# A diagonal recurrence step: product pair and sum on four instructions, rewritten as one product, one reduction and one copy

## What is computed

```python
def s5_direction(u, lam_re, lam_im, log_dt, b_c, h0):
    ...
    a_bar = jnp.exp(lam * dt)
    bu = jnp.einsum('gpc,blgc->blgp', b_bar, u.astype(jnp.complex64))
    bu = bu.at[:, 0].add(a_bar[None] * h0)
    _, h = lax.associative_scan(_lin_combine, (a, bu), axis=1)     # h[t] = a_bar * h[t-1] + bu[t]
    return h
```

## Time and profile before

| | us |
|---|---|
| median of 2 timed runs | 3121.78 (3121.66 to 3121.9) |
| the profiled execution | 3101.36 |
| its span, slowest core (core 0) | 3099.8 |
| spans of the eight cores | 3076.8 to 3099.8 |
| DVE busy, whole span | 1417.5 (46%) |
| ACT busy | 1153.7 (37%) |
| TensorE busy | 1255.5 (41%) |
| POOL busy | 216.6 (7%) |

### The profile page before, as it was taken

How to read it: one execution, slowest core, us unless ns; L and a number is a source line. 1 busy time by engine, 2 the same in 40 slices (tenths; PEclk the granted TensorE clock), 3 DMA queues, 4 the chain that set the end, 5 groups by cost and what they waited for, 6 DMA issues and landing times.

```text
span 3099.8 us, 31698 instructions; the slowest of 8 cores (3076.8 to 3099.8 us)
## 1 busy us (share of the span) xinstructions
PE 1255.5 (41%) x7855; PEld 731.2 (24%) x7855; DVE 1417.5 (46%) x2898; ACT 1153.7 (37%) x1628; POOL 216.6 (7%) x636
## 2 busy tenths in 40 slices
PE   2212162010344646524366706202035463688753
PEld 1211150000223333212132305000032342333332
DVE  1468315666234656275432422566522556523333
ACT  2131524444544343213332333444454534333233
POOL 1000002222000010000000000222200001000000
PEclk9985576565667566667687857556567665699877
DMA  8133210000000100112243241000001011022312
GB/s 210 43 82 82 88 50 31 1 1 1 18 22 12 40 12 31 55 53 70 82 130 105 99 140 45 24 1 1 7 11 31 10 34 37 26 68 75 109 67 96
DMA packets 148798, 162.53 MB, mean 52 GB/s; under 512 B 32872, under 2 KB 124680, under 8 KB 146824
## 3 DMA queue, kind: packets, MB, share of 16 engines
q1 hardware_dynamic: 148616, 160.51, 17.5%
HBM read 119.99 MB, written 40.50 MB: 52 GB/s over the span
## 4 chain that ended last, share of the span: by engine, by line
DVE 32%; PE 25%; issue 14%; DMA 13%; ACT 13%; DVEq 2%; SPq 1%; POOL 1%; ACTq 0%; POOLq 0%
PE ps L1083 7%; DVE T L781 4%; DVE T L779 4%; DVE E L783 4%; ACT wbf L308 3%; PE ps L1086 3%; DVE ors L1041 3%; DMA wst<-w_in 2%; DMA wst<-w_mod 2%; PE ps L1055 2%; PE ps L911 2%; PE ps L901 2%; PE ps L1125 2%; PE ps L702 2%; DVEq L59 2%
## 5 line engine op out<-in xcount | busy, mean ns | idle before, releaser
L782 ACT CAST bufB<-E 128x64 bf16<-128x64 f32 x512 | 242.2, 476 | 318.1 <-DVE T L781 318.0
L1083 PE MATMUL ps<-hT,wbf 128*128 128x512 bf16 x1024 | 263.7, 404 | 172.5 <-ACT wbf L308 169.5
L778 POOL TENSOR_TENSOR T<-E,A 128x64 f32<-128x64 f32 x512 | 163.5, 319 | 1405.9 <-DVE E L776 984.0
L308 ACT CAST wbf<-wst 128x2048 bf16<-128x2048 f32 (+1 forms) x84 | 135.0, 1621 | 213.9 <-DMA wst<-w_in 91.7
L1088 ACT ACTIVATE sg<-ps 128x512 f32<-128x512 f32 x128 | 76.4, 597 | 296.5 <-PE ps L1083 248.9
L759 PE MATMUL ps<-hT,wbf 128*128 128x512 bf16 x256 | 63.7, 415 | 298.6 <-ACT wbf L308 298.6
L1083 PEld LDWEIGHTS ps<-hT,wbf 128*128 128x128 bf16 x1024 | 103.5, 103 | 308.9 <-issue 205.1
L783 DVE TENSOR_TENSOR E<-T,T 128x64 f32<-128x64 f32 x512 | 115.7, 226 | 120.0 <-DVE T L781 87.4
L781 DVE TENSOR_TENSOR T<-T,bufB 128x64 f32<-128x64 f32 x512 | 136.8, 267 | 54.4 <-DVE T L779 1.9
L815 PE MATMUL ps<-GT,bufB 128*128 128x128 bf16 x256 | 43.5, 261 | 284.1 <-ACT Bt L790 284.1
L779 DVE TENSOR_TENSOR T<-E,A 128x64 f32<-128x64 f32 x512 | 116.6, 228 | 54.4 <-DVE E L783 1.9
(11 more groups left out here) (247 smaller groups left out, 2946.7 us busy)
## 6 DMA issues: line engine op xcount, KB each, us to landing
wst<-w_in SPq DMA_DIRECT2D x32, 1024.0 KB, 7.0
wst<-w_mod SPq DMA_DIRECT2D x24, 1024.0 KB, 7.4
xo<-xs_scr SPq DMA_DIRECT2D x8, 2048.0 KB, 10.9
xin<-x SPq DMA_DIRECT2D x16, 512.0 KB, 18.0
xs_scr<-xt SPq DMA_DIRECT2D x4, 2048.0 KB, 12.9
wst<-w_o SPq DMA_DIRECT2D x8, 1024.0 KB, 6.0
xs_scr<-xo SPq DMA_DIRECT2D x4, 2048.0 KB, 17.6
y<-yout SPq DMA_DIRECT2D x16, 512.0 KB, 2.6
```

The lines of the kernel that those rows point to most:

```text
L308: mk.op("act", lambda e: e.copy(bfv, stv), reads=["wst%d" % i], writes=["wbf%d" % j])
L778: mk.op("pool", lambda e, cur=cur: e.tensor_tensor(T1[:], cur, A1[:], ALU.mult), reads=[ck, "A1"], writes=["T1"])
L782: mk.op("act", lambda e, i=i, cur=cur: e.copy(V(Eb, RL, i, [[NR, 64]]), cur), reads=[ck], writes=[ks])
L1083: mk.op("pe", lambda e, ps1=ps1, kt=kt, tt=tt, oc2=oc2, wm=wm: e.matmul(ps1[:], wm[:, kt, oc2 * 128:(oc2 + 1) * 128], hT_ap(kt, tt * 512, ...
```

## The change

The state is kept as three runs of 32 columns, real, imaginary and real again, in `SBF`, so that the swapped state is a window into the same tile that starts 32 columns later. `A12` holds A1 and A2 side by side. One DVE product then makes both products (128 columns) into the first two thirds of `GX`. ACT copies X[i] into the last third (`xprefetch`), one step ahead. A DVE reduction adds the three thirds, and a DVE copy renews the second real run. POOL has no part in the loop any more. The entry blend every 32 steps is followed by the same copy.

```diff
--- before.py
+++ after.py
@@ -736,14 +736,16 @@
                 mk.barrier()
                 dump("Xb", Xb[:], "Xb")
                 ckpt("X")
-                E2 = sb("E2", [128, 128], F32, ph)
-                T1 = sb("T1", [128, 64], F32, ph)
-                T2 = sb("T2", [128, 64], F32, ph)
+                SBF = sb("SBF", [128, 2 * 96], F32, ph)
+                GX = sb("GX", [128, 2 * 192], F32, ph)
+                A12 = sb("A12", [128, 128], F32, ph)
                 EX = sb("EX", [128, NSEG * 64], F32, ph)
                 OST = sb("OST", [128, NSEG * 64], F32, ph)
                 mk.dma(EX[:], s5ext_d.ap()[l], writes=["EX"])
-                memset("dve", E2[:], 0.0, "E2_0")
+                memset("dve", SBF[:], 0.0, "E2_0")
                 mk.bufs["E2_1"] = {"w": mk.bufs["E2_0"]["w"], "r": {}}
+                mk.op("dve", lambda e: e.tensor_copy(A12[:, 0:64], A1[:]), reads=["A1"], writes=["A12"])
+                mk.op("dve", lambda e: e.tensor_copy(A12[:, 64:128], A2[:]), reads=["A2"], writes=["A12"])
                 RL = NR * 64
                 sgtA = [sb("sgtA%d" % i_, [128, 512], BF16, ph) for i_ in range(2)]
 
@@ -763,26 +765,36 @@
                                 yield
 
                 gagen = gate_a_gen()
+
+                def xprefetch(i):
+                    go = (i % 2) * 192
+                    mk.op("act", lambda e, i=i, go=go: e.copy(GX[:, go + 128: go + 192], V(Xb, RL, i, [[NR, 64]])), reads=["Xs%d" % i], writes=["GXx%d" % (i % 2)])
+
+                xprefetch(0)
                 for i in range(NR):
                     if i % max(1, NR // 16) == 0:
                         pump(gagen)
                     kb = i // 32
-                    co = (i % 2) * 64
-                    no = ((i + 1) % 2) * 64
+                    co = (i % 2) * 96
+                    no = ((i + 1) % 2) * 96
+                    go = (i % 2) * 192
                     ck, nk = "E2_%d" % (i % 2), "E2_%d" % ((i + 1) % 2)
-                    cur = E2[:, co:co + 64]
+                    gk, gxk = "GXg%d" % (i % 2), "GXx%d" % (i % 2)
                     ks = "Xs%d" % i
                     if i % 32 == 0:
-                        mk.op("dve", lambda e, cur=cur, kb=kb: e.scalar_tensor_tensor(cur, cur, flags[:, 1:2], EX[:, kb * 64:(kb + 1) * 64], ALU.mult, ALU.add),
+                        mk.op("dve", lambda e, co=co, kb=kb: e.scalar_tensor_tensor(SBF[:, co:co + 64], SBF[:, co:co + 64], flags[:, 1:2], EX[:, kb * 64:(kb + 1) * 64], ALU.mult, ALU.add),
                               reads=[ck, "flags", "EX"], writes=[ck])
-                    mk.op("pool", lambda e, cur=cur: e.tensor_tensor(T1[:], cur, A1[:], ALU.mult), reads=[ck, "A1"], writes=["T1"])
-                    mk.op("dve", lambda e, co=co: e.tensor_tensor(V(T2, 64, 0, [[32, 2], [1, 32]]), V(E2, 128, co + 32, [[-32, 2], [1, 32]]), V(A2, 64, 0, [[32, 2], [1, 32]]), ALU.mult),
-                          reads=[ck, "A2"], writes=["T2"])
-                    mk.op("dve", lambda e, i=i: e.tensor_tensor(T2[:], T2[:], V(Xb, RL, i, [[NR, 64]]), ALU.add), reads=["T2", ks], writes=["T2"])
-                    mk.op("act", lambda e, i=i, cur=cur: e.copy(V(Eb, RL, i, [[NR, 64]]), cur), reads=[ck], writes=[ks])
-                    mk.op("dve", lambda e, no=no: e.tensor_tensor(E2[:, no:no + 64], T1[:], T2[:], ALU.add), reads=["T1", "T2"], writes=[nk])
+                        mk.op("dve", lambda e, co=co: e.tensor_copy(SBF[:, co + 64:co + 96], SBF[:, co:co + 32]), reads=[ck], writes=[ck])
+                    mk.op("dve", lambda e, co=co, go=go: e.tensor_tensor(V(GX, 384, go, [[64, 2], [1, 64]]), V(SBF, 192, co, [[32, 2], [1, 64]]), V(A12, 128, 0, [[64, 2], [1, 64]]), ALU.mult),
+                          reads=[ck, "A12"], writes=[gk])
+                    mk.op("act", lambda e, i=i, co=co: e.copy(V(Eb, RL, i, [[NR, 64]]), SBF[:, co:co + 64]), reads=[ck, gxk], writes=[ks])
+                    if i + 1 < NR:
+                        xprefetch(i + 1)
+                    mk.op("dve", lambda e, no=no, go=go: e.tensor_reduce(SBF[:, no:no + 64], V(GX, 384, go, [[1, 64], [64, 3]]), mybir.AxisListType.X, ALU.add),
+                          reads=[gk, gxk], writes=[nk])
+                    mk.op("dve", lambda e, no=no: e.tensor_copy(SBF[:, no + 64:no + 96], SBF[:, no:no + 32]), reads=[nk], writes=[nk])
                     if (i + 1) % 32 == 0:
-                        mk.op("act", lambda e, kb=kb, no=no: e.copy(OST[:, kb * 64:(kb + 1) * 64], E2[:, no:no + 64]), reads=[nk], writes=["OST"])
+                        mk.op("act", lambda e, kb=kb, no=no: e.copy(OST[:, kb * 64:(kb + 1) * 64], SBF[:, no:no + 64]), reads=[nk], writes=["OST"])
                 drain(gagen)
                 mk.dma(s5o_d.ap()[l], OST[:], reads=["OST"])
                 mk.barrier()
```

## The result

The changed kernel takes 3168.5 us, the median of 11 runs, against 3103.6 us, the median of 10 runs of the kernel before measured with it. The ratio is 1.020, with a 95% interval of 1.016 to 1.024: some 65 us slower. The forecast was slower by 119.6 us. The direction was right, the forecast growth nearly double the measured one. (The base of the forecast, 3121.8 us, was a median of two runs; ten put it at 3103.6, so the growth is what is compared here.) The ratio leaves out slow runs, three of the 11 (3227.9 to 3246.2 us, with a lower granted clock on cores 0 to 3) and one of the 10 before (3150.8 us).

A forecast was written before the change was run, and what follows sets the result against it. The recurrence was taken as bound by DVE's serial chain: +0.225 us a step times 512 gave +115.2, block starts +4.4, together +119.6 us on a base of 3121.8: 3241.4 us, range 3168 to 3268.

The forecast's parts named there:

- What bounds the stage: Recurrence: bound by latency, only DVE's serial chain counts, 1.10 us a step, paid 512 times.
- POOL's removal saves nothing: Recurrence step: POOL's product, 0.32 us, was hidden, so taking it out gains nothing.
- Product 128x128: New DVE product in each step: 292 ns, bounds 228 and 374.
- Reduction: New DVE sum of three thirds: 481 ns, 358 for elements plus 192 x 0.64 for the wide step; bounds 251 and 547.
- The nearest row: Reduction's 481 ns chosen because line 781, same loop and same size, was taken as the nearest trace row.
- Rival B: Reduction not charged for its wide step: 358 ns, step 1.202 us, +56.6 us, 3178.4 us; chance 0.23.
- Copy: New DVE copy of the real half in each step: 170 ns, bounds 164 and 186.
- Gaps: Waits in DVE's chain per step: 0.10 us each before copy and product, 0.17 before reduction, together 0.38 as before.
- ACT hidden: ACT's prefetch of X beside its write-back: worst case 1.15 us, below the 1.325 us step, so it costs 0.
- rival C: Prefetch late behind the gate path's SiLU at 32 places, 0.67 us each: 21 us on top, 3263 us; chance 0.03.
- Block starts, +4.4: At 16 block starts, every 32 steps, one more DVE copy with its gap: +4.4 us.
- The stops for weights: Steps 1 and 129, where a weight load holds ACT and the reduction awaits the prefetch: together zero, within 1 us.

The follow-up runs named there:

- e7: Changed kernel with reduction and prefetch kept, copy and wide product undone, POOL and DVE each making a 64-column product: 3046.5 us in one run against 3098.0 before.
- e9: e7 with the reduction's wait for DVE's own result put last, behind POOL's: recurrences 603.9 us against 569.6.
- e1: Kernel before plus 20 forms of small instructions on scratch tiles, 8 each in a chain of waits; the change's reduction took 19 ns more than adjacent triples.
- e5: Kernel before plus 12 more small-instruction forms, 8 each in a chain of waits; a three-row reduction with outputs 16 bytes apart took 498 ns.
- e2: Changed kernel with each instruction's wait for its own engine put last in the recurrences: 3133.7 us, ratio 1.014 to the kernel before.
- e3: Kernel before with each instruction's wait for its own engine put last in the recurrences: 3065.1 us, ratio 0.992.

## Why the prediction was wrong in size

- *What bounds the stage.* Right. DVE's serial chain is the step, in all versions, with steps from 0.94 to 1.25 us; neither ACT nor POOL bound (but for the four stops for weights and single late steps), except in e7 and e9, where POOL was put on the path. All of the loss lies in the two recurrences.
- *POOL's removal saves nothing.* Nearly right: its product was hidden in 504 of the 512 steps, and in the eight of e9's last rows it held DVE up for 0.25 us each, 2.0 us in all. The product that left it went onto the chain instead.
- *Product 128x128.* 292 forecast, 292 measured.
- *Reduction.* This is the step that failed: 481 forecast, 373 measured. The term was 358 + 192 x 0.64. The 358 for the elements was near (353 contiguous, e1). The surcharge was mis-sized: 19 to 20 ns in place of 123. The price per element was right (0.64 to 0.66 in sums with a second operand 256 or 512 bytes apart, 0.64 in reductions of 4, 6 and 12 rows), but it was applied to a pattern that does not pay it: three rows of adjacent columns come back to the same 16 bytes for four outputs running. In e5 the same three rows without that reuse take 498. 108 ns x 512 = 55.3 us, which with the copy's -5.6 below leaves 49.7 of the miss of 119.6 - 66.4 = 53.2 us in the recurrences; the other 3.5 are 1.5 of gaps (0.382 forecast, 1.225 - 0.846 = 0.379 measured) and the 2.0 of POOL's late steps in the point on the sum.
- *The nearest row.* I called line 781 the nearest because it had the same loop and size. It reads one element of each 16 bytes; the reduction reads four. Line 931, the row against it, was no better: it has 16 elements, on which 0.64 ns each would be 10 ns in all. Rival B, with 358 and 3178.4 us (+56.6), was the case that came, at 0.23; the step it would have been by its terms is 1.202, and 1.225 was measured.
- *Copy.* 170 forecast, 181 measured: 5.6 us more over 512.
- *Gaps.* 0.382 forecast; measured 0.10 to 0.11 for two and 0.17 for the third. Right. That a met wait behind the blocking one costs 0.066 us was read from two rows and holds in e2, e3 and e9, and in the eight late steps of the kernel before.
- *ACT hidden.* Right, and with more room than I gave: the two copies overlap. The prefetch was bounded at 244 to 476; it takes 412. Outside the four stops for weights it has ended at least 0.39 us before the reduction starts (cores 0 and 7), so rival C did not come.
- *Block starts, +4.4.* 16 x 181 ns and 1.7 us of gaps: 4.6. Right.
- *The stops for weights.* Zero within 1 us forecast. The four together cost 26.8 us before and 26.5 after (mean over the cores). Right.
- *Sum by measured terms.* (1.225 - 1.10) x 512 + 4.6 = 68.6 against 66.4 measured. The other 2 us are POOL's late steps. Apart from block starts and stops, 48 of the 512 steps before are over 30 ns longer than the usual 1.10 us and cost 9.3 us together; after, 21 are that much longer than 1.225 and cost 7.3 (starts of lines 779 and 788 on all cores). The eight in which line 783 waits for POOL are 2.0 of the 9.3, and POOL has left the loop. The other 7.3 are in both kernels; why those steps are longer stays open.
- *Luck.* The direction did not hang on it: with 358 for the reduction the sum is slower too. By chance the copy, forecast 5.6 us too low, hid a part of the reduction's 55.3, and the base, 18.2 us too high, added to it: the forecast time is off by 72.9 us, the growth by 54.7.

## What to carry to other kernels

In a chain of small instructions count three things: the instructions in series, the waits that stand behind the one that blocks (0.066 us each here, put the last arrival last, or let an earlier wait cover them), and whether an operand or a reduction comes back to the same 16 bytes. Packing work into fewer, wider instructions pays only if the layout comes for free; here one 32-column copy to keep a layout cost 0.287 us a step, more than twice the whole loss of 0.125. And a row is near to an unknown one when its access pattern is, not when its size is.

## What the runs showed of the hardware

- DVE pays nothing for an fp32 or bf16 operand read every 8 bytes (225 ns for 64 columns), and 42 to 49 ns for any second operand 16 to 512 bytes apart (271 at 16, 274 at 32, 267 at 256 and 512). A reduction over adjacent columns of three rows takes 372 ns for 192 elements against 353 for contiguous ones, over four rows 584 for 256 against an estimated 420 (from 353 and the slope of 1.04 below).
- A wait that is long met costs DVE 0.066 to 0.07 us if it stands behind the one that blocks, and nothing ahead of it: from the last arrival to the start 0.10 us with none behind, 0.17 with one, 0.24 with two (e2, e7, e9, before).
- A reduction over contiguous terms costs per element what a sum does: 353 ns for 192, 553 for 384, a slope of 1.04 ns.
- ACT pays too: 244 ns for 64 contiguous bf16, 297 with a step of 512 bytes (e1, two forms of 8). In the changed kernel's recurrence, where the two overlap, the same read takes 412 and the write-back 514 in place of 476: ACT starts the second 0.15 us after the first (571.50 and 571.65 above).
